# Output blocks of the second layer begun beside the last head's attention

## What is computed

```python
def stick_breaking_branch(h, w_in, w_out):          # 8 heads of 128
    q, k, v, gate = jnp.split(h @ w_in, 4, axis=-1)
    def block(args):                                # 128 queries
        z = jnp.einsum('bhqd,bhsd->bhqs', q_blk, k) * scale
        log_1m = jnp.where(mask, jax.nn.log_sigmoid(-z), 0.0)
        tail = lax.cumsum(log_1m, axis=3, reverse=True) - log_1m
        A = jnp.where(mask, jnp.exp(jax.nn.log_sigmoid(z) + tail), 0.0)
        return jnp.einsum('bhqs,bhsd->bhqd', A, v)
    return (o * jax.nn.silu(gate)) @ w_out          # the product of this case

# reference: h = h + stick_breaking_branch(u, ...); return rmsnorm(h, final_norm_w)
```

## Time and profile before

| what | us |
|---|---|
| median of 3 executions | 1495.12 (1494.43 to 1496.27) |
| the profiled execution's own time | 1495.06 |
| its span in the profile | 1491.9 |
| head 7's attention on PE to the first of the 342 products | 1348.68 to 1393.29 |
| the 342 products | 1393.29 to 1472.84 |
| the norm and the stores | 1472.84 to 1491.9 |

### The profile page before, as it was taken

One profiled execution on the slowest core, in us unless ns is written; L12 is line 12 of the kernel. 1 busy time (PEld: TensorE's weight loads), 2 busy tenths in 40 slices (PEclk: granted clock), 3 DMA queues, 4 the chain that ended last, 5 costly groups with the idle time before them and its releaser, 6 DMA issues.

```text
span 1491.9 us, 18475 instructions
## 1 busy us (share of the span) xinstructions
PE 1396.9 (94%) x7351; PEld 1146.8 (77%) x7351; DVE 901.9 (60%) x1532; ACT 641.6 (43%) x879; POOL 441.7 (30%) x230
## 2 busy tenths in 40 slices
PE   5898999999999999997996989999999999997897
PEld 4687787888888888876884768778787878776685
DVE  6387787869686878677336135555545455567313
ACT  6253435253535353543224234545454445546213
POOL 6443334323333343335214411221112121221120
PEclk9999999999999999998999999999999999999999
DMA  7110110101111111030111210111110100000302
GB/s 190 52 31 27 29 36 22 50 22 36 36 36 29 36 36 35 20 113 22 64 54 43 71 29 29 29 43 29 29 29 29 43 29 29 29 29 0 113 29 112
DMA packets 97190, 65.20 MB, mean 44 GB/s; under 512 B 2401, under 2 KB 91602, under 8 KB 97106
## 3 DMA queue, kind: packets, MB, share of 16 engines
q1 hardware_dynamic: 97106, 64.04, 14.4%
HBM read 53.54 MB, written 10.49 MB: 43 GB/s over the span
## 4 chain that ended last, share of the span: by engine, by line
PE 80%; DVE 12%; ACT 3%; issue 2%; POOL 1%; DMA 0%; POOLq 0%; SPq 0%; DVEq 0%; PEldq 0%; ACTq 0%
PE psum L407 51%; PE psum L1715 4%; PE psum L1741 4%; DVE terms L1288 3%; PE psum L1664 3%; PE psum L1675 3%; PE psum L1728 2%; PE psum L1610 2%; PE psum L1635 2%; PE psum L1656 1%; DVE stick L1405 1%; PE psum L1619 1%; DVE small_L L1273 1%; PE psum L1561 1%; DVE Xs L1281 1%
## 5 line engine op out<-in xcount | busy, mean ns | idle before, releaser
L407 PE MATMUL psum<-u_hi,w_hi 128*128 128x512 f32 x1264 | 523.5, 414 | 27.2 <-DVE u_lo L1068 7.0
L407 PE MATMUL psum<-u_lo,w_hi 128*128 128x512 f32 x1264 | 517.1, 409 | 0.0
L407 PE MATMUL psum<-u_hi,w_lo 128*128 128x512 f32 x1264 | 506.7, 401 | 0.0
L380 POOL TENSOR_TENSOR w_lo<-w_raw,w_hi 128x1024 fp32r<-128x1024 f32 (+1 forms) x83 | 212.0, 2555 | 713.8 <-ACT w_hi L375 713.8
L407 PEld LDWEIGHTS psum<-u_hi,w_hi 128*128 128x128 f32 x1264 | 240.5, 190 | 82.9 <-issue 21.5
L407 PEld LDWEIGHTS psum<-u_lo,w_hi 128*128 128x128 f32 x1264 | 240.7, 190 | 49.7 <-issue 7.2
L407 PEld LDWEIGHTS psum<-u_hi,w_lo 128*128 128x128 f32 x1264 | 240.3, 190 | 49.9 <-issue 3.8
L375 ACT ACTIVATE w_hi<-w_raw 128x1024 fp32r<-128x1024 f32 (+1 forms) x83 | 85.8, 1034 | 159.2 <-PE psum L407 104.4
L702 POOL TENSOR_TENSOR Lb<-dec,level 128x512 f32<-128x512 f32 x64 | 97.8, 1544 | 126.0 <-PE psum L1664 68.7
L1157 DVE SCALAR_TENSOR_TENSOR late<-raw,cols,late 128x1024 f32<-128x1024 f32 x72 | 123.2, 1710 | 1.9
L1009 ACT ACTIVATE soft<-psum 128x1024 f32<-128x1024 f32 (+3 forms) x64 | 41.7, 652 | 161.3 <-DVE psum L1393 160.7
(11 more groups left out here) (202 smaller groups left out, 2053.7 us busy)
## 6 DMA issues: line engine op xcount, KB each, us to landing
w_raw<-in_a_w_in SPq DMA_DIRECT2D x33, 512.0 KB, 4.1
w_raw<-in_b_w_in SPq DMA_DIRECT2D x32, 512.0 KB, 4.0
x_stage<-in_x SPq DMA_DIRECT2D x8, 512.0 KB, 7.4
w_raw<-in_b_w_out SPq DMA_DIRECT2D x8, 512.0 KB, 3.6
out<-fin_o SPq DMA_DIRECT2D x8, 512.0 KB, 2.6
resid<-late SPq DMA_DIRECT2D x6, 512.0 KB, 3.2
o_rows<-o_nrm SPq DMA_DIRECT2D x12, 256.0 KB, 2.0
w_raw<-in_a_w_out SPq DMA_DIRECT2D x8, 384.0 KB, 3.1
```

The costliest lines, as they stand in the source:

```text
L380: G.tensor_tensor(tiles(w_lo, key), tiles(w_raw, key), tiles(w_hi, key).bitcast(F32), ALU.subtract).then_inc(lo_done, 1)
L407: mm = PE.matmul(psum[:, half], (w_hi, w_hi, w_lo)[part][:, n % 2, k], (u_hi, u_lo, u_hi)[part][:, k, half * HALF:(half + 1) * HALF], star ...
```

## The change

The first three output blocks get keys of their own (`"pre"`), over heads 0 to 6 alone: 7 x 6 = 42 products each, 126 in all. They are put into head 7's attention by a list with four counts a step, `LAST_FILL`. What they lack, head 7, is added by a block `"fin"` of 3 x 6 = 18 products ahead of the last output block. The upper parts of heads 0 to 6 are made by ACT in steps 0 (three), 1 (two) and 2 (two), and the lower parts by POOL instead of DVE. DVE adds the finished blocks within attention. The upper and lower part of head 7 are made before the common border, and DVE writes the latter. The weights of output block 3 are loaded and split before the border too; the first load behind it is that of block 4. The output blocks 3 to 7 (`"out"`) are full ones, and only their products on head 7 wait for its lower part.

```diff
+PRE = 3
+LAST_FILL = ((0, 2, 2, 8), (4, 4, 4, 6), (4, 4, 4, 6), (4, 4, 3, 6), (4, 4, 0, 8), (5, 3, 0, 8), (6, 2, 0, 6),
+             (5, 4, 3, 3))
+SPLIT_AT = {0: (0, 1, 2), 1: (3, 4), 2: (5, 6)}
...
-        SEQ += [("b", h, b) for h in range(H) for b in range(4)] + [("out", cb) for cb in range(KB)]
+        SEQ += [("b", h, b) for h in range(H) for b in range(4)] + [("pre", cb) for cb in range(PRE)]
+        SEQ += [("out", cb) for cb in range(PRE, KB - 1)] + [("fin", 0), ("out", KB - 1)]
...
+                if key == ("pre", 0) and half == 0 and part == 0:
+                    PE.wait_ge(ob_lo, k + 1)
+                if key[0] == "out" and k == H - 1 and part == 0:
+                    PE.wait_ge(ol_lo, 5)
...
+        def fin_group(i):
+            cb, half, key = i // 2, i % 2, ("fin", 0)
+            PE.wait_ge(lo_done, NUMBER[key] + 1)
+            PE.wait_ge(proj_taken, FIRST[key] + i - 1)
+            for part in range(3):
+                mm = PE.matmul(psum[:, half], tiles((w_hi, w_hi, w_lo)[part], key)[:, cb],
+                               (u_hi, u_lo, u_hi)[part][:, H - 1, half_range(half)], start=part == 0, stop=part == 2)
+            mm.then_inc(proj_ready, 1)
+        PRE_AT = [sum(sum(LAST_FILL, ())[:n]) for n in range(4 * NC + 1)]
+        def pre_products(first, last):
+            for cb in range(PRE):
+                size = 6 * (H - 1)
+                lo, hi = max(first - cb * size, 0), min(last - cb * size, size)
+                if lo < hi:
+                    products(("pre", cb), lo, hi)
...
@@ SP
-            for b in range(2):
-                load_w(sp, ("out", b), wbo_v[:, :, b * P:(b + 1) * P])
+            for cb in range(PRE):
+                load_w(sp, ("pre", cb), wbo_v[:, 0:H - 1, cb * P:(cb + 1) * P])
+            load_w(sp, ("out", PRE), wbo_v[:, :, PRE * P:(PRE + 1) * P])
             arrive(sp)
             all_arrived(sp, 3)
...
-            for n in range(2, KB):
-                load_w(sp, ("out", n), wbo_v[:, :, n * P:(n + 1) * P])
+            for cb in range(PRE + 1, KB):
+                if cb == KB - 1:
+                    load_w(sp, ("fin", 0), wbo_v[:, H - 1, 0:PRE * P].rearrange("p (c m) -> p c m", m=P))
+                load_w(sp, ("out", cb), wbo_v[:, :, cb * P:(cb + 1) * P])
@@ POOL
+            for k in range(H - 1):
+                pool.wait_ge(ob_hi, k + 1)
+                G.tensor_tensor(u_lo[:, k, :], o_all[:, k, :], u_hi[:, k, :].bitcast(F32), ALU.subtract
+                                ).then_inc(ob_lo, 1)
+            split_lo(("pre", 2))
+            split_lo(after_next(("pre", 1)))
             arrive(pool)
@@ ACT, attend
-                    if not follow and s < H - 1:
-                        output_upper(s)
+                    if not follow:
+                        for k in SPLIT_AT.get(s, ()):
+                            output_upper(k)
+                        if s == 4:
+                            split_hi(("pre", 2))
+                        if s == 7:
+                            split_hi(after_next(("pre", 1)))
...
             attend(H - 1, False)
+            output_upper(H - 1)
             arrive(act)
             all_arrived(act, 3)
-            output_upper(H - 1)
@@ DVE, attend
-                    if not follow and s < H - 1:
-                        output_lower(2, s)
+                    if not follow:
+                        for cb, half in pre_ended(s):
+                            add_block(("pre", cb), cb, half)
...
             attend(H - 1, False)
+            dve.wait_ge(ob_hi, H)
+            V.tensor_tensor(u_lo[:, H - 1, :], o_all[:, H - 1, :], u_hi[:, H - 1, :].bitcast(F32), ALU.subtract
+                            ).then_inc(ol_lo, 1)
             arrive(dve)
@@ PE, attend
+                    if not follow:
+                        pre_products(pre[0], pre[1])
                     if s == 0:
                         transpose_v(h, 0)
                     transpose_a(h, s, 0)
                     fill.to(after_first)
+                    if not follow:
+                        pre_products(pre[1], pre[2])
                     if s >= 1:
                         weigh(h, s - 1)
-                    if not follow and s >= 1:
-                        products(("out", 0), 6 * s - 6, 6 * s)
                     fill.to(after_sums)
+                    if not follow:
+                        pre_products(pre[2], pre[3])
                     if s == 0:
                         transpose_v(h, 1)
                     transpose_a(h, s, 1)
                     if s == NC - 1:
                         weigh(h, s)
                     fill.to(step_end)
+                    if not follow:
+                        pre_products(pre[3], pre[4])
@@ PE, behind attention
-            products(("out", 0), 6 * KB - 6, 6 * KB)
-            for cb in range(1, KB):
+            for cb in range(PRE, KB):
+                if cb == KB - 1:
+                    for i in range(2 * PRE):
+                        fin_group(i)
                 products(("out", cb), 0, 2 * MMS)
```

More of the change, by code:

```diff
@@ L235, in build @@
         o_out, o_back = [sem(f"o_out{i}") for i in range(2)], [sem(f"o_back{i}") for i in range(EARLY)]
+        ob_hi, ob_lo = sem("ob_hi"), sem("ob_lo")
         oe_hi, oe_lo, ol_hi, ol_lo = sem("oe_hi"), sem("oe_lo"), sem("ol_hi"), sem("ol_lo")
@@ L345, in build @@
             FIRST[key] = n_groups
-            n_groups += 8 if key[0] == "last" else 2
+            n_groups += 8 if key[0] == "last" else 2 * PRE if key[0] == "fin" else 2
             FREED[key] = n_groups
@@ L351, in heads_of @@
         def heads_of(key):
-            return EARLY if key[0] == "early" else 2 if key[0] == "last" else KB
+            return {"early": EARLY, "last": 2, "pre": H - 1, "fin": PRE}.get(key[0], KB)
         def tiles(t, key):
@@ L385, in after_next @@
             return SEQ[NUMBER[key] + 2]
-        U_ROUND = {"gate": 0, ("b", 0, 0): 1, ("out", 0): 2}
-        BY_K = ("gate", ("z", H - 1), ("early", 0), ("b", 0, 0), ("out", 0))
+        U_ROUND = {"gate": 0, ("b", 0, 0): 1}
+        BY_K = ("gate", ("z", H - 1), ("early", 0), ("b", 0, 0), ("pre", 0))
         def products(key, first, last):
@@ L427, in last_group, with pre_ended @@
             mm.then_inc(proj_ready, 1)
+        def fin_group(i):
[7 more added lines that the diff above has]
+        PRE_AT = [sum(sum(LAST_FILL, ())[:n]) for n in range(4 * NC + 1)]
+        assert PRE_AT[-1] == PRE * 6 * (H - 1)
+        def pre_products(first, last):
[4 more added lines that the diff above has]
+                    products(("pre", cb), lo, hi)
+        def pre_ended(s):
+            size = 6 * (H - 1)
+            return [(cb, half) for cb in range(PRE)
+                    for half, end in enumerate((size - 3 if cb == 0 else size // 2, size))
+                    if PRE_AT[4 * s] < cb * size + end <= PRE_AT[4 * s + 4]]
         def in_all(fill):
@@ L764, in _ @@
                 serve_b(h)
+            for k in range(H - 1):
[4 more added lines that the diff above has]
+            split_lo(after_next(("pre", 1)))
             arrive(pool)
             all_arrived(pool, 3)
-            for cb in range(KB - 2):
-                split_lo(("out", cb + 2))
+            for key in SEQ[NUMBER["pre", 2] + 2:]:
+                split_lo(key)
         @block.scalar
@@ L793, in output_upper @@
                 if k == 0:
-                    act.wait_ge(proj_ready, FIRST["out", 0])
-                A.activation(u_hi[:, k, :], o_all[:, k, :], ACT.Copy).then_inc(u_hi_done, 1)
+                    act.wait_ge(proj_ready, FIRST["pre", 0])
+                bo_done.wait(act, k, 2)
+                A.activation(u_hi[:, k, :], o_all[:, k, :], ACT.Copy).then_inc(ob_hi, 1)
             def take(key, half, dst):
@@ L1042, in _ @@
             attend(H - 1, False)
+            output_upper(H - 1)
             arrive(act)
             all_arrived(act, 3)
-            output_upper(H - 1)
-            for cb in range(KB - 2):
-                act.wait_ge(proj_taken, FIRST["out", cb] + 2)
-                split_hi(("out", cb + 2))
+            for key in SEQ[NUMBER["pre", 2] + 2:]:
+                split_hi(key)
             for n in range(NC):
@@ L1070, in u_lower, with add_block @@
                                        ).then_inc(u_lo_done, 1)
[L1072 to L1076, removed]
+            def add_block(key, cb, half):
+                n = FIRST[key] + half + (2 * cb if key[0] == "fin" else 0)
+                if cb >= HOME:
+                    dve.wait_ge(late_in, 32 * (KB - HOME))
+                dve.wait_ge(proj_ready, n + 1)
+                V.tensor_tensor(xT(cb)[:, half_range(half)], psum[:, half], xT(cb)[:, half_range(half)], ALU.add
+                                ).then_inc(proj_taken, 1)
             def rms_by_tokens(rnd):
@@ L1470, in _ @@
             attend(H - 1, False)
+            dve.wait_ge(ob_hi, H)
```

(6 more changed lines are left out.)

## The result

The changed kernel takes 1512.86 us (median of 4, 1512.33 to 1514.36) against 1494.78 for the kernel before (median of 4). The ratio is 1.0121, 95% interval 1.0106 to 1.0136: slower by 18.1 us where 14.6 were forecast. The profiled execution took 1512.33, its span is 1510.6, which is 18.7 us more than the span before. It is the fastest of the four, with the highest mean granted clock (0.979; the others had 0.976 to 0.977).

A forecast was written before the change was run, and what follows sets the result against it. The prediction took TensorE (PE) to bound the kernel, busy 94% of the span. Attention +30.3 us and the part behind it -15.7 us gave +14.6 on 1495.06: 1509.7, said as 1510, range 1502 to 1518.

The forecast's parts named there:

- That PE is the bound and only idle time matters: Whole kernel: TensorE busy 94% of the span; with the number of products unchanged, only filling idle time can win.
- The three stalls: Steps 0 to 2 of head 7's attention: PE waits for lower parts from POOL, 5.8, 8.1 and 5.9 us.
- Attention's end: Head 7's attention: ends 30.3 us later than before, at about 1421 us.
- The half clock behind the stalls: PE work after each long stall in attention: slowed by 1.3 us each, +4.0 us.
- PE's work in steps 3 to 7: Head 7's attention, from step 3's scores to the gating's end: PE's queue full, 26.3 us.
- Behind attention: From the last gating's end to the end of the kernel: 66.4 us instead of 82.1, a gain of 15.7 us.
- The wait for block 4: After block 3, behind the border: PE waits 5.3 us for block 4's later-loaded weights.
- The clock behind it: After PE's wait for block 4's weights: 1.6 us of half clock again.
- `fin`: Ahead of the last output block: 18 products, 4.1 us, plus 0.8 us for DVE emptying two banks.
- The rule on VectorE and GpSimd: Steps 1 to 4: two-input DVE and SBUF-reading GpSimd instructions exclude each other; new subtractions and scans do not meet.
- the rival: Head 7's attention: four scans do meet POOL's subtractions, about 1.4 us each, 5.6 us on top: 1515; chance 8%.
- The faster rival: Steps 0 to 2: lower parts arrive ahead of PE, 84 products only fill gaps, attention ends as before: 1479; chance 7%.

The follow-up runs named there:

- e3_fill: The changed kernel with the same 126 products put later in head 7's attention, each behind its split: 1492.33 us, ratio 0.999 to the kernel before.
- e1_silu: The changed kernel with ScalarE making the upper parts of heads 3 and 4 ahead of the gate's Silu and table loads: 1510.68 us.
- e2_load: The changed kernel with block 4's weights loaded ahead of the common border instead of behind it: 1505.63 us.
- e5_splits_only: The kernel before with only the change's splits (upper parts earlier, lower parts of heads 0 to 6 on GpSimd), products unmoved: 1491.39 us.
- e4_fill_load: The changed kernel with both the later products of e3_fill and the earlier load of e2_load: 1485.32 us.
- e9_later_load: The same kernel as e4_fill_load, run again beside another kernel on the same chip: 1484.14 us.

## Why the prediction was right

**That PE is the bound and only idle time matters.** Right. The products are the same in number, and what was added is idle time and half clock.

**The three stalls.** Forecast 5.8, 8.1 and 5.9 us, measured 5.73, 7.98 and 5.71, in front of the products named, released by POOL's `u_lo`. The second is a little lucky: its own terms (1368.2 + 1.05 + 2.37) give 1371.6, not 1371.4, and a stall of 8.3. e3_fill shows that they are the cause: the same instructions behind their splits give 20.5 us back. PE's waits for GpSimd fell by 17.0 us, the half clock behind them (5.3 us) went, and 3.4 us of other waits came back (v's copy 2.6, an Exp 0.8). e1_silu shows that the Silu and its tables, ahead of the splits, were 3.8 us of the second stall.

**Attention's end.** From the mask on, the forecast stood at 70.8 us (1350.16 to 1421), measured 73.1. Two terms of the sum were too small. The half clock behind the stalls came to 5.3 us of loss (half of 2.8, 3.8 and 3.9 us of PE work) where I had set 4.0. And PE's work in steps 3 to 7, from step 3's scores (1395.96) to the gating's end (1423.12), took 27.2 us instead of 26.3. Together they are 2.2 of the missing 2.3 us. For the work I priced each product at its distance to the next product, 0.23. A product that follows another kind of matmul takes more, as the timeline of PE in the changed kernel shows:

```profile
1398.90 1.50 PE L1793 MATMUL psum<-aT,b_v 128*128 128x128 f32 x12
1400.15 0.48 PE L420 MATMUL psum<-u_hi,w_lo 128*128 128x512 f32 x1
...
1400.47 0.39 PE L420 MATMUL psum<-u_hi,w_hi 128*128 128x512 f32 x1
1400.70 0.39 PE L420 MATMUL psum<-u_lo,w_hi 128*128 128x512 f32 x1
```

The first of the group is 0.32 from its neighbour, the next 0.23, and in the timeline the 78 products of steps 3 to 7 stand in 15 groups. 15 times 0.09 is 1.3 us, so by this estimate the spacing alone covers the 0.9.

**Behind attention.** Forecast -15.7, measured -13.7. The wait for block 4 was 4.83 for 5.3. The clock behind it was the term that was mis-sized: I took 1.6 us as before, but it stayed at half for longer (5.3 us of PE work at 0.50, from 1439.37), and 144 products took 35.47 instead of 32.7, 2.8 us. `fin` took 5.65 instead of 4.9 (1474.65 to 1480.30), as every second group waits 0.2 to 0.3 for DVE and starts anew. The norm and the stores, costed as unchanged, took 19.4 instead of 19.0. e2_load confirms the wait and its clock as one cost of 7.2 us.

**The rule on VectorE and GpSimd.** In the changed kernel the new subtractions and the scans of steps 1 to 4 did not meet, as forecast: the scans took 1.75, 1.48 and 1.21, their lengths alone. They met as soon as the stalls were gone, so the condition that the rival named was right. Its price of 5.6 us was too high: not four scans met but two, and they waited 1.9 us in e3_fill and 3.8 in e5_splits_only.

**The faster rival.** It would have needed the lower parts ahead of PE. e4_fill_load makes that so and lands at 1485, not 1479, because attention then takes 14 us longer than before, not the same time. The rival's "84 products only fill gaps" was too good: of their 19.1 us, 5.1 found a gap there and 6.7 in e3_fill (A of 54.6 and 53.0 against 40.6), and e5_splits_only has 2.3 of it from the splits alone. The 16.7 us of waiting that the prediction counted were not all room for products, since 3.3 of them lie behind the gating, where PE waits for head 7's split. The rival's condition was also put too low: from 30.3 to 15.7 is 14.6 us, three quarters of the 19.8 us of stalls and not half. e3_fill removed 17 of them, and came out 2.0 us below the kernel before.

What was not tried: head 0's lower part ahead of the weight split on GpSimd, and a list of its own for each order on ScalarE.

## What to carry to other kernels

Work put into the gaps of an in-order engine must stand behind its inputs in time; a product that is one step too early does not fill a gap, it holds up everything queued behind it, here the transposes that feed the engine that makes its input. Moving work ahead of a common border also moves the border: ask which loads start behind it, and whether the cover ahead of their use got shorter. And once the gaps are full, each further product only changes its place: the last 42 saved 1.4 to 3 us of their 9.5.

## What I had not expected of the hardware

The same idle time was followed by different amounts of PE work at 1.2 GHz: behind the first stall, 5.73 and 5.72 us long and reached by the same instructions, 2.8 us in the changed kernel and 4.3 in e1_silu. Even two executions of one kernel differ. e4_fill_load and e9_later_load both have 2.62 us of idle time ahead of v's second transposes in step 0, and then short ones. The first has two stretches at half clock in its attention, the second none (the windows are A, columns as in the earlier trace rows):

```profile
1350.96:1405.59 54.63, 49.05 (x254) 40.09 (x252) 31.95 (x48) 26.39 (x38) 27.14 (x10) 0.94 0.07 20
```

```profile
1348.24:1401.25 53.01, 46.49 (x254) 37.80 (x252) 31.51 (x48) 26.40 (x38) 28.42 (x10) 1.00 0.07 20
```

The wait for block 4 (4.83 us) cost 2.8 us of clock where the 3.3 us ahead of the row of products before had cost 1.6. A forecast that prices stalls alone leaves this out. Here the half clock was 1.3 us short behind the three stalls and 1.2 us short behind block 3, of an error of 3.5 us in all. What decides between a short and a long slow stretch behind the same idle time stays open.
